# The relative-bias table of a decoder layer made between the turning of the two row tiles, with its three inputs among the first loads

## What is computed

```python
h = rmsnorm(x, g_mix[l])
proj = h @ w_in[l]                                   # 1024 -> 2816 columns
pa, pb, pc, pd = jnp.split(proj, ...)                # four token mixers
...                                                  # scores + head_bias(tab, dist) in three of them
merged = sum_i sigmoid(h @ w_gate[l, i]) * (branch_i @ w_br[l, i])
x = x + merged @ w_o[l]
x = x + hierarchical_moe(rmsnorm(x, g_ffn[l]), ...)  # top-2 of 32 gated experts
return rmsnorm(x, g_final)

def head_bias(tab, dist):                            # tab (heads, 32 buckets)
    return jnp.take(tab, rel_bucket(dist), axis=1)
```

## Time and profile before

| what | value |
|---|---|
| time, median of 3 runs | 700.39 us |
| the three runs | 700.39, 699.29, 701.89 us |
| the profiled execution's own time | 700.59 us |
| its span, first to last instruction | 698.7 us |
| PE busy | 673.4 us (96%) |
| DVE busy | 248.8 us (36%) |
| ACT busy | 190.8 us (27%) |
| mean DMA rate | 349 GB/s |

### The profile page before, as it was taken

The page is one execution under the profiler, slowest core; times in us unless marked ns, Lnnn a source line. Parts: engine busy times, 40 slices in busy tenths (PEclk is TensorE's granted clock), DMA queues, the critical chain, the costliest instruction groups (busy, mean ns, idle before and its releaser), DMA issues.

```text
span 698.7 us, 9817 instructions
## 1 busy us (share of the span) xinstructions
PE 673.4 (96%) x3998; PEld 390.0 (56%) x3998; DVE 248.8 (36%) x534; ACT 190.8 (27%) x295; POOL 3.6 (1%) x8
## 2 busy tenths in 40 slices
PE   8999999998999999999999999899999899898995
PEld 6999777776777844434444444344344343453433
DVE  6663677667787662111111112121121110210213
ACT  6434566688654511001001011011010100100112
POOL 0010000000000000000000000000000000000000
PEclk9999999999999999999999999999999999999998
DMA  9897651293679999999999999999999999999993
GB/s 335 290 307 231 239 173 45 87 317 103 181 248 408 412 357 364 424 409 431 427 425 428 425 427 425 425 426 428 427 427 425 428 425 429 426 426 418 418 394 115
DMA packets 47526, 243.71 MB, mean 349 GB/s; under 512 B 10432, under 2 KB 13688, under 8 KB 34040
## 3 DMA queue, kind: packets, MB, share of 16 engines
q1 hardware_dynamic: 46600, 241.12, 87.0%
q0 software_dynamic: 448, 1.59, 0.6%
q10 hardware_dynamic: 432, 0.33, 0.2%
HBM read 241.96 MB, written 1.07 MB: 348 GB/s over the span
## 4 chain that ended last, share of the span: by engine, by line
PE 77%; DMA 13%; DVE 5%; ACT 2%; issue 2%; SPq 0%; DVEq 0%; ACTq 0%
PE bank L1861 28%; DMA unit<-in_w 12%; PE bank L1925 11%; PE bank L1496 7%; PE bank L1497 7%; PE bank L1498 7%; PE bank L1840 5%; PE bank L1939 2%; PE bank L1940 2%; DVE low L353 1%; PE bank L1872 1%; DMA x<-in_x 1%; PE bank L1899 1%; PE bank L1646 1%; PE bank L1750 1%
## 5 line engine op out<-in xcount | busy, mean ns | idle before, releaser
L1861 PE MATMUL bank<-unit,xT 128*64 128x512 f32 x1008 | 229.8, 601 | 11.5 <-DMA unit<-in_w 8.3
L1861 PEld LDWEIGHTS bank<-unit,xT 128*64 128x64 f32 x1008 | 75.4, 138 | 149.8 <-issue 147.8
L1925 PE MATMUL bank<-unit,hidT 128*64 128x512 f32 x480 | 106.3, 595 | 0.0
L1496 PE MATMUL bank<-high,hT_hi 128*128 128x512 f32 (+2 forms) x208 | 79.6, 383 | 1.9 <-DVE low L353 1.6
L1497 PE MATMUL bank<-low,hT_hi 128*128 128x512 f32 (+2 forms) x208 | 77.4, 372 | 0.0
L353 DVE TENSOR_TENSOR low<-unit,high 128x2048 fp32r<-128x2048 f32 (+1 forms) x34 | 70.8, 2100 | 17.5 <-ACT high L348 17.5
L1925 PEld LDWEIGHTS bank<-unit,hidT 128*64 128x64 f32 x480 | 33.1, 137 | 61.5 <-issue 60.0
L348 ACT ACTIVATE high<-unit 128x2048 fp32r<-128x2048 f32 (+1 forms) x34 | 59.0, 1756 | 23.2 <-DMA unit<-in_w_in 13.5
L1498 PE MATMUL bank<-high,hT_lo 128*128 128x512 f32 (+2 forms) x176 | 65.1, 370 | 0.0
L1365 DVE TENSOR_TENSOR y_lo<-bank,y_hi 128x512 fp32r<-128x512 f32 x30 | 20.8, 692 | 94.1 <-ACT y_hi L876 94.1
L857 ACT ACTIVATE sg<-bank,slot_rs 128x512 f32<-128x512 f32 x16 | 11.0, 687 | 147.8 <-DVE slot_rs L1328 147.8
(11 more groups left out here) (262 smaller groups left out, 666.5 us busy)
## 6 DMA issues: line engine op xcount, KB each, us to landing
unit<-in_w SPq DMA_DIRECT2D x78, 2048.0 KB, 26.4
unit<-in_w SPq DMA_DIRECT2D x26, 1024.0 KB, 10.3
unit<-in_w_gate SPq DMA_DIRECT2D x8, 2048.0 KB, 10.5
unit<-in_w SPq DMA_DIRECT2D x10, 512.0 KB, 18.8
unit<-in_w_in SPq DMA_DIRECT2D x2, 2048.0 KB, 16.2
unit<-in_w_o SPq DMA_DIRECT2D x2, 2048.0 KB, 11.4
unit<-in_w_in SPq DMA_DIRECT2D x6, 512.0 KB, 7.1
unit<-in_w_in SPq DMA_DIRECT2D x3, 1024.0 KB, 10.2
```

The lines of the kernel that those rows point to most:

```text
L1496: mm(dst, a_hi, b_hi, start=first, stop=False)
L1861: last = mm(bank[4 + w][g * CAP:(g + 1) * CAP, :], xT[:, k, g * CAP:(g + 1) * CAP], up_rows(slots[2 * w + g], k), start=(k == 0), stop=(k ...
L1925: last = mm(bank[6 + n][g * CAP:(g + 1) * CAP, :], hidT[:, c, g * CAP:(g + 1) * CAP], rhs[:, c, n * BANK:(n + 1) * BANK], start=(c == 0), ...
```

## The change

The three inputs of the bias table leave SP's `small_loads` and are issued by ACT, right behind `gmix`, on one semaphore with it. The product that makes the table moves from before block 10 to between the eight transposes of row tile 0 and the eight of row tile 1, into bank 1, which is free then. DVE adds the mask before it splits the first weights. PE waits for `dvec` before the first projection product, because block 1 writes bank 1. POOL's write to DRAM keeps its late place by a wait for ten finished blocks. ACT's wait for `gmix` becomes a wait for all four loads.

```diff
             def small_loads():
-                sp.dma_start(relb[:], a["rel_bias"]).then_inc(s["small"], 16)
-                sp.dma_start(onehot[:], a["bucket_onehot"]).then_inc(s["small"], 16)
-                sp.dma_start(bmask[:], a["bias_mask"]).then_inc(s["small"], 16)
...
             pool.wait_ge(s["dvec"], 1)
+            pool.wait_ge(s["proj"], 10)
             pool.dma_start(dram_vec, dvec[:]).then_inc(s["scratch"], 16)
...
-            act.dma_start(gmix[:], a["g_mix"][0].rearrange("(p k) -> p k", k=KD)).then_inc(s["gmix_in"], 16)
+            act.dma_start(gmix[:], a["g_mix"][0].rearrange("(p k) -> p k", k=KD)).then_inc(s["firsts"], 16)
+            act.dma_start(onehot[:], a["bucket_onehot"]).then_inc(s["firsts"], 16)
+            act.dma_start(relb[:], a["rel_bias"]).then_inc(s["firsts"], 16)
+            act.dma_start(bmask[:], a["bias_mask"]).then_inc(s["firsts"], 16)
             act.wait_ge(s["warm"], 3)
             link(nc.scalar.activation(warm, warm, ACT.Sqrt))
             high_part(act, 0, 0)
-            act.wait_ge(s["gmix_in"], 16)
+            act.wait_ge(s["firsts"], 16 * 4)
...
             sum_of_squares(0)
+            dve.wait_ge(s["firsts"], 16 * 4)
+            dve.wait_ge(s["table"], 1)
+            nc.vector.tensor_tensor(dvec[:], bank[1][0:12, 0:MAP], bmask[:], ALU.add).then_inc(s["dvec"], 1)
...
-            def bias_vectors():
-                dve.wait_ge(s["small"], 16 * 9)
-                dve.wait_ge(s["table"], 1)
-                nc.vector.tensor_tensor(dvec[:], bank[7][0:12, 0:MAP], bmask[:], ALU.add).then_inc(s["dvec"], 1)
-
             def constants():
+                dve.wait_ge(s["small"], 16 * 6)
...
             for t in range(NT):
+                if t:
+                    pe.wait_ge(s["firsts"], 16 * 4)
+                    mm(bank[1][0:12, 0:MAP], relb[:], onehot[:], start=True, stop=True).then_inc(s["table"], 1)
                 pe.wait_ge(s_x[t], 16)
...
+            pe.wait_ge(s["dvec"], 1)
             for quarter in range(4):
...
             for i in range(ends[0], len(blocks)):
-                if i == 10:
-                    pe.wait_ge(s["small"], 16 * 9)
-                    evacuated(pe, 7)
-                    mm(bank[7][0:12, 0:MAP], relb[:], onehot[:], start=True, stop=True).then_inc(s["table"], 1)
...
-                if i == 15:
-                    pe.wait_ge(s["dvec"], 1)
```

More of the change, by code:

```diff
@@ L278, in hybrid_decoder_layer @@
         slot_no = cst[:, C_SLOT:C_SLOT + CAP]
-        names = """cst small wr late scratch biasT tr1 dvec lam_of gmix_in proj projA projD scores sread norm probs
+        names = """cst small wr late scratch biasT tr1 dvec lam_of firsts proj projA projD scores sread norm probs
             maps logs ptps dd pt gate tanh pv oev bsq brms ob oTps oTs br mrg bf x1 second_half norms row_norms queries_two squared
@@ L944, in _ @@
             sum_of_squares(0)
+            dve.wait_ge(s["firsts"], 16 * 4)
+            dve.wait_ge(s["table"], 1)
+            nc.vector.tensor_tensor(dvec[:], bank[1][0:12, 0:MAP], bmask[:], ALU.add).then_inc(s["dvec"], 1)
             for j in range(4):
                 low_part(dve, nc.vector, 0, j)
-                if j == 0:
-                    dve.wait_ge(s["gmix_in"], 16)
                 dve.wait_ge(s["hTh"], j + 1)
@@ L1001, in _ @@
                                                        op0=ALU.mult, op1=ALU.mult).then_inc(s["projD"], 1)
-                if u == 2:
-                    bias_vectors()
                 for half in range(2 if u < 5 else 0):
```

## The result

| | median | lowest to highest | runs |
|---|---|---|---|
| before | 700.46 us | 699.26 to 703.0 | 22 |
| changed | 702.25 us | 699.94 to 705.45 | 22 |

The ratio is 1.0022, with a 95% interval of 1.0013 to 1.0031. That is 0.9 to 2.2 us slower, where 0.25 us faster was forecast. The time lies inside the range given (698.7 to 702.6), and the difference is within the 0.5% that the prediction took for no change, but it has the other sign.

What follows compares the result with a forecast made beforehand. PE work was taken to bound the chain to 67.23 us, DMA the late experts, starting when PE lets it. -0.74 at block 10 + 0.49 at the start = -0.25 us: median 700.1, range 698.7 to 702.6.

Steps and rivals of the forecast that it cites:

- The gain at block 10: On PE at 37.94 us: without the table's product, block 10 follows block 9 at once, 0.74 us less.
- F = 5.81 + 1.3 = 7.1: Start: F, landing of the last of three loads, 1.3 us behind `gmix`; row tile 1's transposes 0.49 us late.
- the break-even of 7.35: Start of PE's row tile 1 transposes: from F = 7.35 on, the start loses more than the 0.74 us gained.
- the lower bound: Start: the three loads land with `gmix` at 5.81; row tile 1 is pushed back only 0.2 us; sum -0.54 us.
- the first rival: Before row tile 1's transposes: loads land late and hold PE, slower than before; chance 0.14.
- Its price of 2.75: Late loads holding PE at the start: with the last landing at 10.1, 2.75 us slower, 703.1 us.
- The rule that went with it: DMA queues at the start: an engine empties a whole packet from one queue before turning, so small loads wait for SP's.
- The 2.0 us: Loads at the start: about 2.0 us fixed cost per DMA, `bmask` landing near 4.6; not used.
- DVE, ACT and the queues further on: Mask addition, ACT's extra issuing and later queues: no cost; bias copies about 3.4 us earlier, gaining nothing.
- The shift carries to the end: From PE before 250 us through the experts: a shift reaches the end one for one.
- a shift lost on the way: Experts' DMA stream starts at its own pace, not PE's: no change, 700.4 us; chance 0.09.
- an ACT issue stalled for 7.55 us: ACT's issues at the start stall: `bmask` lands at 14.3, PE 7.7 us late, time 707.3; chance 0.04.

Runs made afterwards that it cites:

- e9: The change run again without edit, against the kernel before: 2.1 us slower (1.3 to 2.9), mean clock 0.9909 against 0.9924.
- e5: The change with eight warm-up products on PE before its wait for the four loads: 1.1 us slower than the kernel before (0.4 to 1.8).
- e2: The kernel before with twelve warm-up products instead of one ahead of the first projection product: 2.7 us slower (1.8 to 3.6).
- e11: The change with PE also waiting for weight piece 2, filled with 17 warm-up products: 2.9 us slower than the kernel before (1.8 to 4.1).
- e1: The kernel before with five warm-up products instead of one ahead of the first projection product: +0.4 us (-0.3 to +1.1).
- e3: The kernel before with the three loads issued by ACT behind gmix, table's product left before block 10: 0.8 us slower (0.3 to 1.5).
- e10: The change with PE also waiting for weight piece 2 before the table's product, standing idle: 5.3 us slower than the kernel before (4.1 to 6.5).
- e6: The kernel before with the three loads issued by ACT, product unmoved, eight warm-up products before PE's wait for row tile 1: 1.5 us slower (0.8 to 2.2).

## Why the prediction was wrong

**The gain at block 10** was right in kind and a little small: 0.74 forecast, 0.91 found. Block 10's first product, 0.2 longer behind the table's product (0.32 against 0.12), had been left out.

**The landing of the loads failed: "My estimate is F = 5.81 + 1.3 = 7.1".** `bmask` landed at 8.17 (2.66 + 5.51), beyond the break-even of 7.35. Two sizes in it were off. ACT's queue moved 118 packets between 5.5 and 7.5 us in the changed kernel:

```profile
q1 hardware_dynamic: 237, 0.68, 92.6%
q10 hardware_dynamic: 118, 0.07, 11.6%
```

The count of 124 was nearly right (120: ACT's queue moved 408 packets in all, against 288 before); the time was 0.27 us for each of some 7.4 per engine and not 0.17. The 0.17 came from a stretch in which 1.4 of SP's packets went by for each of ACT's (411 to 288); here it was two. And the landing was reported 0.7 us after the last packet, where `gmix` had needed 0.4. A smaller term was short as well: row tile 1 took 6.3 us to land instead of 5.6, where the lower bound had pushed it back by 0.2. With `bmask` at 7.1 the transposes would have started at 8.0, behind row tile 1, and not at 7.84. So the first rival, late loads that hold PE, was the right one, at the place that it named. Its price of 2.75 stood for a landing at 10.1; by the same sum 8.17 gives +0.82, and 0.66 was found. The rule that went with it (the Trainium skill, DMA: Bandwidth & Descriptors, section Queues, rings and completion order), a whole packet from one queue before the next, isn't settled by these counts: the queues didn't alternate one for one, but `bmask` didn't wait for the whole of piece 1 either, which was issued before it and landed at about 9.2 in the changed kernel (2.18 + 7.0).

The 2.0 us that the prediction took from the Trainium skill (DMA: Bandwidth & Descriptors, section Anatomy of one DMA) and set aside stand there for DMAs that GpSimd issues. ACT issues these, and nothing in the forecast rests on the 2.0.

**A term was missing: what PE's idle time does to its clock.** The prediction treated PE's idle time as empty room. In the change it grew from 1.35 to 2.21 us in one profile; it was 1.32 in another, in which row tile 0's transposes had themselves started late. In some executions the granted clock then falls to 0.50 for about 3 us, at a price of 1.1 us in e9 against the first profile. How often: the mean clock is 0.0018 and 0.0015 below that of before in the two sets, which at a clock of 0.50 is 0.0018 x 698 / 0.5 = 2.5 us and, likewise, 2.1 us of time at 0.50 per execution; with some 3.5 us for one fall that is an estimate of six or seven executions in ten. Then 0.66 + 0.65 x 1.1 = 1.4 us, inside the measured 0.9 to 2.2 and at the low end of e9's 1.3 to 2.9.

The single runs point the same way. Of the 33 runs of the change 16 have a mean clock of 0.990 or less, of the 86 of the kernel before beside the experiments 7. In the result's 22 runs the eleven low ones have a median of 703.13 us and the eleven others 700.77; in the kernel before a low mean clock goes with no such rise (700.59 against 700.17). By these runs a fall goes with some 1.6 to 2.4 us, more than the 1.1 between the two profiles. So that the clock takes a part is shown; its exact size in the change, and the remainder in e5 and in the better runs of e9 (1.1 and 1.3 us where the chain shows 0.7), are not.

The Trainium skill, in TensorE: Matmul & The Clock Gate, section Part 1: The HAM clock gate, says that the clock is set by how busy PE has been lately, and that the same kernel can come out differently from run to run; these traces agree, with 1.00 in one profile of the change and 0.50 in another. The clock bore on this change, and the prediction left it out. What decides in a single execution whether the clock falls stays open, and the mean clock of a single run doesn't tell it for certain: the profiled run of e9 had 0.992 with the fall in it, and the expert stage has falls of its own (0.98 from 535 to 690 us before).

**DVE, ACT and the queues further on** cost nothing, as forecast, though the transfers moved by other amounts. DVE added the mask in 0.55 us and PE waited at most 0.16 us ahead of L1531. POOL's write moved from 41.60 to 40.16 and its copies by 5.2 us, from 49.47 to 44.31 and from 50.40 to 45.24, where 3.4 was forecast; the first copy thus went out 0.4 us ahead of the landing of the sixth weight unit's last part (37.79 + 6.9 = 44.7), not behind it, and the chain shows no wait for either. The first use of the bias at 74.92 was as little bound by them as the one at 74.26:

```profile
40.16 0.70 POOL L649 DMA_DIRECT2D dram_vec<-dvec  x1 [39.70 <-PE bank L1497]
44.31 0.94 POOL L652 DMA_DIRECT2D bias_ab<-dram_vec  x1 [3.45 <-DMA dram_vec<-dvec]
45.24 0.76 POOL L653 DMA_DIRECT2D bias_d<-dram_vec  x1
```

**The shift carries to the end**, as the prediction argued from the 341 GB/s at 252 us; e2 and e11 show it for shifts of 2.55 and 3.03 us at ACT's rounding, which came out as 2.7 and 2.9; e1's 0.44, which came out as 0.4, is too small to show it alone. One reading of the early chain was loose: between 7.93 and 8.78 it ran through ACT's `hT_hi` and not through PE, which changes none of the sums. The rivals of a shift lost on the way and of an ACT issue stalled for 7.55 us fall: `bmask` took 0.89 us to issue.

## What to carry to other kernels

A gap on an engine that waits for a DMA is no free room for work with an input of its own, until that input is shown to land before the gap ends: here 0.74 us of work cost 1.6 at the start, because it stood in order ahead of what had set the end. Time a small load at the start by its place in the stream behind other transfers, with the packet rate of the stretch in which it will move. And where TensorE waits longer than it did, count what it loses at half its clock behind the wait, in the executions in which that happens, and look at the mean clock of all runs, since one profile may show the other kind.

## What the runs showed of the hardware

Idle times of PE of 1.3 to 1.9 us were followed in some executions by a granted clock of 0.50 (e9, e3); one of 1.35 (the profile before) and one of 2.2 (the first profile of the change) were not; in one of 4.0 the clock was at 0.50 before PE started again (e10, 0.51 from 9 to 10 us). The fall can come late: in e9 it lies near 9.6 us, when PE had been busy again since 8.13.

A small load issued from a second queue took 5.5 us to land for 18 KB while the other queue kept the DMA engines busy (a share of 92.6% from 5.5 to 7.5 us).

The start itself scatters: the transposes of row tile 0 began between 4.84 and 5.32 us in these profiles. The clock column doesn't show all of it. It reads 1.00 from the start, yet in the chain of e6 the ten warm-up products at the start took 4.45 us and the eight later ones 1.73, so PE went at half the pace there, 0.45 us each against 0.22:

```profile
1.08 4.45 PE bank L1478 x10
...
7.17 1.73 PE bank L1478 x8
```
